# A hybrid decoder layer on eight cores: convolution gathered from a DRAM scratch, first weight slab requested first, norm two tiles ahead

## The chip, the cores and the metric

The kernel runs on all 8 cores of one Trainium2 chip. Each core has a matmul engine (TensorE, PE in the profile), VectorE (DVE), ScalarE (ACT), GpSimd (POOL) and SyncE (SP), and 16 DMA engines. There is no traffic between cores. The time is the device time of the slowest core, in microseconds. A comparison counts as faster or slower from 2% on.

## The reference

One layer of a decoder trunk, for 2 prompts of 8192 tokens and for 128 requests of 4 new tokens, D = 2048:

```python
n = _rmsnorm(hp, norm1_g[l])
q, k, v, u, g = _project(n, w_in[l], b_gate[l])        # u = ua * sigmoid(ub), gates = sigmoid
ya = _prompt_attention(q, k, v, sink[l])               # window 128, blocks of 128, sink column
ubuf = jnp.pad(u, ((0, 0), (CONV_W - 1, 0), (0, 0)))   # 31 taps, depthwise, 1024 channels
yc = _conv_tail(ubuf, conv_w[l], conv_b[l], cln_g[l], cln_b[l], w_conv_o[l])
hp = _finish(hp, ya, yc, g, w_attn_o[l], w_out[l], norm2_g[l], w_up[l], w_down[l])
...
def _finish(x, y_att, y_conv, gates, w_attn_o, w_out, norm2_g, w_up, w_down):
    ya = y_att @ w_attn_o
    mix = (gates[..., 0, :] * ya + gates[..., 1, :] * y_conv) @ w_out
    h = x + mix
    z = _rmsnorm(h, norm2_g) @ w_up
    return h + jnp.square(jax.nn.relu(z)) @ w_down
```

The sample requests go through the same steps, with cached keys, values and 30 cached convolution inputs each. The outputs are the final RMS norm of both, and the caches moved on by the new tokens.

## The kernel before

Each core computes 2048 prompt tokens and 64 sample tokens, channels on the partitions and tokens in the free dimension. It goes through them in three groups: 5, 6 and 5 blocks of 128 tokens; the first has a halo of 128 tokens more, the last the 64 sample tokens. A group passes through all layers before the next begins. The weights come anew for every group, in slabs of 2048 rows by 512 columns (2 MB in bf16, converted by the transfer), through three buffers `w0` to `w2`; `load_slab` requests the slab two ahead on GpSimd's queue when a stage begins. A slab serves 8 column tiles of 16 matmuls (`dense`), over two halves of the group's tokens (320, 384 and 352 columns in the three groups).

The stages of a group: `phase1` (RMS norm of the input, tile by tile, to `N`), `ua`, `kv`, `q`, `ub` (projections, of which `ua` and `ub` make the gated convolution input `u` in region `R2`), attention in units woven between these, then `conv_stage` woven between the first gate projections, `mix`, `out`, four pairs `up`/`dn` of the MLP, and `fin_stage`. All engines take their instructions in program order; `run(main, side, per)` sets that order by hand: after each step of the main stage it lets the side stage advance by `per` steps. Semaphore waits are derived from what each instruction reads and writes; `place` says which tiles of a region lie over which.

The convolution multiplies, per channel block of 128, a tile `X` with small weights `wd`: four groups of 32 channels, each with four shifted copies of `u` on the partitions, so that 8 matmuls cover 32 taps. `load_x` fills `X` by DMA from `u`, on SyncE's queue: 16 transfers per channel block, or 32 in the last group, where the sample tokens' `XS` comes too. `X` has four buffers, or two in the last group. `c`, the result, lies over `u` in region `R2`.

`phase1` of a later group runs beside the last down-projection, `dn_stage(G, 3)`, of the group before. Its step `front` squares an input tile (ScalarE), multiplies it by the norm's weights (GpSimd) and, in later groups, sums the squares over 16 blocks by halving (VectorE, into `ring`); its step `back` sums over partitions by a matmul with `onesD`, then takes root, reciprocal and product to `nT`. In the first group `back` sums by 16 matmuls of full width instead. The same down-projection also accumulates the squares of `h` for the final norm (`acc_stat`: ScalarE squares, GpSimd adds into `nS`).

The input copies that are outputs too (`ksn`, `vsn`, `csn`: caches shifted by four tokens) are requested in `consts`, on SyncE's queue, near the start.

## Time and profile before

| | us |
|---|---|
| median of 3 runs | 3978.87 |
| lowest, highest | 3974.25, 4410.77 |
| profiled execution, own time | 3986.84 |
| its span (slowest core, core 0) | 3985.4 |
| spans of the eight cores | 3947.3 to 3985.4 |
| TensorE busy | 3512.2 (88%) |
| VectorE, ScalarE, GpSimd busy | 1100.6, 879.9, 658.7 |
| matmuls in the chain that ended last | 72% |

The profile is of one execution, of the core that took longest. TensorE's busy time counts its matmuls at whatever clock was granted to it, so a busy stretch can still be slow. Every line of the program's work is recorded under one source line, L130, so groups are told apart by the names of their tiles: `MIX<-R` is the gather of `u` (in `R2`) into `X` (in `MIX`), `ps<-MIX,wd` are the convolution's matmuls, `ring` are the norm's sums.

### The profile page before, as it was taken

How to read it: one execution, taken by the hardware profiler on the slowest of the kernel's cores; microseconds unless marked ns; L12 is line 12 of the kernel's file. 1: busy time of each engine (PE TensorE's matmuls, PEld its weight loads, DVE VectorE, ACT ScalarE, POOL GpSimd, SP SyncE). 2: the span in 40 equal slices, each digit the busy share in tenths (PEclk: the TensorE clock that was granted, in tenths of full speed). 3: DMA queues.
4: the chain of work that ended last, by engine and by line, in shares of the span. 5: the costliest groups of instructions: out<-in, count | busy, mean ns of one | idle time of the engine just before them, and what ended most of it. 6: DMA issues, size and time to landing. Idle time of an engine off the chain costs nothing.

```text
span 3985.4 us, 62687 instructions; the slowest of 8 cores (3947.3 to 3985.4 us)
## 1 busy us (share of the span) xinstructions
PE 3512.2 (88%) x24352; PEld 2254.2 (57%) x24352; DVE 1100.6 (28%) x1936; ACT 879.9 (22%) x1955; POOL 658.7 (17%) x625
## 2 busy tenths in 40 slices
PE   3976999999988986999999999898535999999997
PEld 3644677677655543566666665464323666666664
DVE  2232222222245432312222222535203122222223
ACT  1243113100113343113210010314203113101103
POOL 3124012000023124003000001411112012000004
PEclk7998999999988998999999999788867999999998
DMA  8754689988876654569777677594423789888874
GB/s 157 115 99 85 97 149 141 124 115 125 120 137 140 105 92 79 76 97 165 103 104 98 99 106 118 97 171 69 90 69 51 106 145 130 108 110 117 106 110 97
DMA packets 389906, 440.98 MB, mean 111 GB/s; under 512 B 13584, under 2 KB 371600, under 8 KB 387216
## 3 DMA queue, kind: packets, MB, share of 16 engines
q0 software_dynamic: 347696, 355.68, 63.9%
q1 hardware_dynamic: 41920, 81.30, 7.2%
q8 instruction: 198, 3.24, 0.3%
q14 instruction: 92, 0.75, 0.1%
HBM read 752.81 MB, written 23.86 MB: 195 GB/s over the span
## 4 chain that ended last, share of the span: by engine, by line
PE 72%; SPq 6%; DVE 6%; ACT 5%; DMA 5%; issue 4%; POOL 0%; DVEq 0%; ACTq 0%; POOLq 0%
PE ps L130 72%; SPq L130 6%; DMA w<-w_up 3%; DVE R L130 2%; DVE MIX L130 2%; ACT TMP L130 2%; ACT P L130 1%; ACT R L130 1%; DVE TMP L130 1%; DMA MIX<-xf 1%; DMA wd<-wdx 1%; ACT MIX L130 1%; DMA w<-w_in 0%; DVE sm L130 0%; DVE GT L130 0%
## 5 line engine op out<-in xcount | busy, mean ns | idle before, releaser
L130 PE MATMUL ps<-N,w 128*128 128x384 bf16 (+3 forms) x11712 | 1809.3, 317 | 28.8 <-DMA w<-w_in 16.6
L130 PEld LDWEIGHTS ps<-N,w 128*128 128x128 bf16 x11712 | 1148.1, 99 | 681.3 <-issue 69.6
L130 PE MATMUL ps<-MIX,w 128*128 128x320 bf16 (+2 forms) x4608 | 688.8, 313 | 0.0
L130 PEld LDWEIGHTS ps<-MIX,w 128*128 128x128 bf16 x4608 | 450.9, 98 | 236.5
L130 PE MATMUL ps<-GT,w 128*128 128x320 bf16 (+2 forms) x3072 | 489.7, 325 | 0.0
L130 PEld LDWEIGHTS ps<-GT,w 128*128 128x128 bf16 x3072 | 311.3, 101 | 175.2 <-issue 10.0
L130 DVE SCALAR_TENSOR_TENSOR ring<-ps,TMP 128x320 f32<-128x320 f32 (+2 forms) x384 | 201.2, 525 | 703.9 <-PE ps L130 701.3
L130 DVE TENSOR_TENSOR R<-ps,R 128x320 f32<-128x320 f32 (+2 forms) x384 | 200.2, 524 | 636.5 <-PE ps L130 636.1
L130 PE MATMUL ps<-R,w 128*128 128x320 bf16 (+2 forms) x1536 | 261.3, 333 | 80.3 <-ACT GT L130 39.4
L130 PEld LDWEIGHTS ps<-R,w 128*128 128x128 bf16 x1536 | 155.8, 103 | 184.3 <-issue 101.4
L130 POOL TENSOR_TENSOR TMP<-TMP 128x320 f32<-128x320 f32 (+5 forms) x201 | 202.4, 1007 | 298.2 <-ACT TMP L130 295.6
L130 PE MATMUL ps<-MIX,wd 128*32 128x320 bf16 (+2 forms) x1792 | 87.3, 367 | 167.2 <-DMA MIX<-R 119.5
L130 ACT ACTIVATE TMP<-R 128x320 f32<-128x320 f32 (+5 forms) x264 | 136.1, 516 | 431.4 <-DVE R L130 422.0
L130 ACT ACTIVATE GT<-ring 128x320 bf16<-128x320 f32 (+2 forms) x192 | 95.3, 496 | 599.4 <-DVE ring L130 599.4
L130 ACT ACTIVATE MIX<-ring 128x320 bf16<-128x320 f32 (+2 forms) x192 | 94.9, 496 | 591.4 <-DVE ring L130 591.3
L130 DVE SCALAR_TENSOR_TENSOR GT<-GT,ps 128x320 f32<-128x320 f32 (+2 forms) x192 | 99.9, 520 | 402.7 <-PE ps L130 394.0
L130 ACT ACTIVATE GT<-ps,hbg 128x320 f32<-128x320 f32 (+2 forms) x192 | 106.1, 553 | 448.0 <-PE ps L130 448.0
L130 POOL DMA_DIRECT2D w<-w_dn x48 | 55.0, 1146 | 815.5 <-PE ps L130 815.5
L130 POOL DMA_DIRECT2D w<-w_up x48 | 55.3, 1152 | 703.1 <-PE ps L130 703.1
L130 PEld LDWEIGHTS ps<-MIX,wd 128*32 128x32 bf16 x1792 | 57.1, 119 | 197.9 <-issue 175.3
L130 ACT ACTIVATE P<-TMP,sm 128x129 bf16<-128x129 f32 (+1 forms) x264 | 107.9, 409 | 149.4 <-DVE sm L130 131.6
L130 POOL DMA_DIRECT2D w<-w_in x45 | 52.8, 1174 | 433.1 <-PE ps L130 396.2
(96 smaller groups left out, 1668.9 us busy)
## 6 DMA issues: line engine op xcount, KB each, us to landing
w<-w_up POOLq DMA_DIRECT2D x48, 2048.0 KB, 22.2
w<-w_dn POOLq DMA_DIRECT2D x48, 2048.0 KB, 17.0
w<-w_in POOLq DMA_DIRECT2D x45, 2048.0 KB, 16.8
w<-w_ac POOLq DMA_DIRECT2D x12, 2048.0 KB, 15.8
w<-w_out POOLq DMA_DIRECT2D x12, 2048.0 KB, 22.6
MIX<-xf SPq DMA_DIRECT2D x17, 1024.0 KB, 8.2
MIX<-R SPq DMA_DIRECT2D x256, 41.8 KB, 1.9
MIX<-R SPq DMA_DIRECT2D x128, 49.8 KB, 2.6
```

Source lines behind the costliest of these rows:

```text
L130: ins = getattr(engobj, fn[0])(*fn[1], **fn[2])
```

## The change

1. **Gather.** A stage `ub_stage` that has finished four channel blocks writes them to a DRAM scratch, `uscr` (`sscr` for the sample tokens). `load_x` reads from there, one transfer per shift for all four groups of channels: 4 per channel block, 8 in the last group. The first two `wd` are requested after the first `q` stage, and in the first two groups the loads of `X` are queued before attention's last units.
2. **Start.** The first weight slab is requested before the first tile is multiplied, the second after it; the constants and the cache copies come later.
3. **Norm.** `phase1` keeps three input buffers in all groups and a buffer for the squares of its own, in `AT`, a new tile that also holds attention's `P` and `PT`. `front` is two tiles ahead of `back`. In the first group every second tile is summed by halving.
4. **Cache copies** stand behind `up(1)` of groups 0 and 1.
5. **Final norm.** In groups 0 and 1 half of the additions of `acc_stat` move to VectorE, and the scale `gf` moves from ScalarE into VectorE's final multiplication. In the last group the last slab of the down-projection does all first halves before the second, and the first half's final norm starts under it. Outputs leave in stores of 2 or 4 channel blocks.

```diff
         def load_slab():
...
+        def prefetch(n):
+            while slab_at[1] < min(n, len(slabs)):
...
         def phase1(G):
-            place("MIX", [(f"x{i}", i * 8192, (i + 1) * 8192) for i in range(nx)] + ([] if first else [("xsq", 16384, 24576)]))
+            place("MIX", [(f"x{i}", i * 8192, (i + 1) * 8192) for i in range(3)])
+            place("AT", [("sq0", 0, 8192)])
...
-                if not first:
+                if not (first and i % 2 == 0):
                     for hw in (8, 4, 2, 1):
...
-            for i in range(min(nx, nt)):
+            for i in range(3):
                 load(i)
+            yield
             front(0)
+            yield
+            front(1)
             yield
             for i in range(nt):
                 back(i)
-                if i + nx < nt:
-                    load(i + nx)
+                if i + 3 < nt:
+                    load(i + 3)
                 yield
-                if i + 1 < nt:
-                    front(i + 1)
+                if i + 2 < nt:
+                    front(i + 2)
                     yield
...
         def ub_stage(G, hf):
+            hs = slice(hf * 4, hf * 4 + 4)
+            dmas("sp", [(uscr[G.g, hs, :, 0:G.UW].rearrange("k p c -> p k c"), G.uT[:, hs, :])],
+                 reads=[f"uT{c}" for c in range(hf * 4, hf * 4 + 4)], writes=[f"us{hf}"], sem=f"d_us{hf}")
...
             def load_x(ch):
                 i = ch % nb
                 pairs = []
-                for g in range(4):
-                    for tap in range(4):
-                        pairs.append((X[i][32 * tap:32 * tap + 32, g, :], G.uT[32 * g:32 * g + 32, ch, 1 + tap:1 + tap + L]))
...
+                for tap in range(4):
+                    src = uscr[G.g, ch].rearrange("(g c) w -> c g w", c=32)[:, :, 1 + tap:1 + tap + L]
+                    pairs.append((X[i][32 * tap:32 * tap + 32, :, :], src))
...
-        def acc_stat(G, src, rk, c, first):
+        def acc_stat(G, src, rk, c, first, dn=False):
+            eng = "dve" if dn and c else "pool"
...
+                    if G.last and fb == 3 and cb == 3 and c == 1:
+                        if mm_ == 1:
+                            fin_stat(G, 0)
+                        elif mm_ == 2:
+                            fin_rows(G, 0, 0, 4)
+                        elif mm_ == 3:
+                            fin_rows(G, 0, 4, 16)
...
-        for j in (1, 2):
-            slab_dep[j] = ["x0", "x1", "x2"]
+        slab_dep[1] = ["x0", "x1", "x2"]
         ph = phase1(Gs[0])
         next(ph)
+        prefetch(1)
+        next(ph)
+        prefetch(2)
+        drain(ph)
         consts()
-        drain(ph)
...
             dense_banks(4)
+            conv = conv_stage(G)
+            next(conv)
             att = att_stage(G)
...
+            if not G.SA:
+                next(conv)
             drain(att)
-            conv = conv_stage(G)
+            if G.SA:
+                next(conv)
...
+            if G.g == 0:
+                dmas("sp", [(ksn[:, :, :], ck[:, 4:128, :])], sem="d_o1")
+            if G.g == 1:
+                dmas("sp", [(vsn[:, :, :], cv[:, 4:128, :]), (csn[:, :, :], st[:, 4:30, :])], sem="d_o1")
```

GpSimd's order at the start, the piece of the difference (`w` are the weight slabs, `MIX<-MIX,vec` the multiplications of the six input tiles):

```order
-L130 TENSOR_TENSOR MIX<-MIX,vec 128x2048
+L130 DMA w<-w_in 128x16x512
+L130 TENSOR_TENSOR MIX<-MIX,vec 128x2048
+L130 DMA w<-w_in 128x16x512
+L130 TENSOR_TENSOR MIX<-MIX,vec 128x2048 x5
 L130 DMA msk<-masks 128x512
 L130 DMA smk<-smask 128x264
 L130 DMA idb<-ident 128x128
-L130 TENSOR_TENSOR MIX<-MIX,vec 128x2048 x5
-L130 DMA w<-w_in 128x16x512 x6
```

Two slabs move ahead of the multiplications, and the constants behind them.

SyncE's queue in the last group, from the attention's last transfers to the first channel block's gather, before:

```order
L130 DMA v_o<-GT 128x256
L130 DMA vs_o<-GT 64x256
L130 DMA MIX<-R 1x8x256 x8
L130 DMA u_o<-GT 128x768
L130 DMA MIX<-R 32x668
L130 DMA MIX<-R 32x512
```

and now:

```order
L130 DMA MIX<-R 1x8x256 x8
L130 DMA uscr<-R 128x4x672
L130 DMA sscr<-R 128x4x560
L130 DMA uscr<-R 128x4x672
L130 DMA sscr<-R 128x4x560
L130 DMA u_o<-GT 128x768
L130 DMA MIX<-uscr 32x4x668
L130 DMA MIX<-sscr 32x4x512
```

The pair `MIX<-R 32x668`, `32x512` stood there 128 times, the pair `MIX<-uscr`, `MIX<-sscr` stands 32 times, and the scratch writes stand ahead of the first.

VectorE's order in the norm stretch of the first group, one tile, before (`R<-ps,R` are the down-projection's additions, `MIX<-MIX` the halvings of the squares):

```order
L130 TENSOR_TENSOR MIX<-MIX 128x1024
L130 TENSOR_TENSOR MIX<-MIX 128x512
L130 TENSOR_TENSOR MIX<-MIX 128x256
L130 TENSOR_TENSOR ring<-MIX 128x128
L130 TENSOR_TENSOR R<-ps,R 128x320 x2
L130 RECIPROCAL ring<-ring 128x128
L130 TENSOR_TENSOR N<-MIX,ring 128x16x128
```

and now:

```order
L130 RECIPROCAL ring<-ring 128x128
L130 TENSOR_TENSOR N<-MIX,ring 128x16x128
L130 TENSOR_TENSOR R<-ps,R 128x320 x2
L130 TENSOR_TENSOR TMP<-TMP 128x320
L130 TENSOR_TENSOR AT<-AT 128x1024
L130 TENSOR_TENSOR AT<-AT 128x512
L130 TENSOR_TENSOR AT<-AT 128x256
L130 TENSOR_TENSOR ring<-AT 128x128
```

The halvings now belong to the tile two behind the one whose reciprocal stands ahead of them, and an addition of the statistics (`TMP<-TMP`) has joined every two additions of `h`.

## Rows read from the trace of the kernel before

**Rows 1.** Waits of TensorE, core 0: who was waited for; us in total, times, longest.

```profile
PE ps L130 <- DMA MIX<-R: 119.5, 11, 20.4
...
PE ps L130 <- DVE ring L130: 60.1, 12, 6.4
...
PE ps L130 <- DMA wd<-wdx: 24.3, 2, 12.2
```

**Rows 2.** Timeline, 0 to 100 us: start, us, engine, operation [idle before <-releaser].

```profile
2.92 0.88 SPq L130 DMA_DIRECT2D ksn<-ck  x1
...
11.05 1.91 ACT L130 ACTIVATE GT<-MIX 128x2048 f32<-128x2048 f32 x1
...
34.45 2.29 DVE L130 TENSOR_TENSOR N<-MIX,ring 128x2048 bf16<-128x2048 f32 x1
...
55.52 1.91 ACT L130 ACTIVATE GT<-MIX 128x2048 f32<-128x2048 f32 x1 [22.24 <-DMA MIX<-xf]
...
76.88 3.52 POOL L130 DMA_DIRECT2D w<-w_in  x3
...
93.98 6.20 PE L130 MATMUL ps<-N,w 128*128 128x336 bf16 x24 [16.59 <-DMA w<-w_in]
```

**Rows 3.** Timeline of the last group's gather, then that tile's requests and landings.

```profile
2832.19 169.21 SPq L130 DMA_DIRECT2D MIX<-R  x256
...
2855.70 4.89 PE L130 MATMUL ps<-MIX,wd 128*32 128x320 bf16 x96 [20.37 <-DMA MIX<-R]
...
2876.84 4.71 PE L130 MATMUL ps<-MIX,wd 128*32 128x320 bf16 x96 [13.67 <-DMA MIX<-R]
...
L130 SPq DMA_DIRECT2D MIX<-R x40: 507/591/1323, 2832.2 to 2859.4; - x40
...
DMA to landing us min/median/max: 1.8/5.4/6.2
```

**Rows 4.** Timeline of the first group's convolution.

```profile
291.52 4.46 PE L130 MATMUL ps<-MIX,wd 128*32 128x320 bf16 x64 [12.11 <-DMA wd<-wdx]
...
298.87 2.36 PE L130 MATMUL ps<-MIX,wd 128*32 128x320 bf16 x64
```

**Rows 5.** Timeline of the two norm stretches (1130 us, 2465 us), then 1181 us.

```profile
1171.50 10.36 PE L130 MATMUL ps<-GT,w 128*128 128x320 bf16 x64
...
1188.00 0.76 PE L130 MATMUL ps<-ring,onesD 128*128 128x128 f32 x2 [6.14 <-DVE ring L130]
...
2510.07 12.37 PE L130 MATMUL ps<-GT,w 128*128 128x384 bf16 x64
...
1181.69 5.77 DVE L130 TENSOR_TENSOR MIX<-MIX 128x1024 f32<-128x1024 f32 x3 [3.58 <-ACT MIX L130]
...
1181.73 4.65 POOL L130 TENSOR_TENSOR MIX<-MIX,vec 128x2048 f32<-128x2048 f32 x1 [1.53 <-ACT MIX L130]
```

**Rows 6.** Timeline of the end.

```profile
3929.72 25.97 PE L130 MATMUL ps<-GT,w 128*128 128x352 bf16 x173
...
3958.16 4.57 DVE L130 RECIPROCAL TMP<-TMP 128x352 f32<-128x352 f32 x2 [1.78 <-ACT TMP L130]
...
3962.64 16.16 DVE L130 TENSOR_TENSOR R<-R,TMP 128x352 f32<-128x352 f32 x22
```

**Rows 7.** Stretches: busy us by engine, clock, DMA share, GB/s; last row core 2.

```profile
550.00:700.00 150.00, 150.00 (x1103) 107.94 (x1101) 43.42 (x82) 44.67 (x95) 36.06 (x39) 1.00 0.97 152
...
1650.00:2450.00 800.00, 800.00 (x4921) 481.65 (x4920) 181.67 (x319) 123.96 (x233) 73.22 (x68) 1.00 0.75 110
...
2600.00:2650.00 50.00, 50.00 (x287) 31.46 (x286) 22.85 (x40) 11.01 (x24) 6.97 (x7) 0.81 0.88 191
...
2600.00:2650.00 50.00, 50.00 (x352) 34.57 (x351) 25.25 (x46) 11.27 (x25) 8.85 (x9) 1.00 0.92 194
```

**Rows 8.** Requests: KB each, median us to landing.

```profile
ksn<-ck SPq DMA_DIRECT2D x1, 1984.0 KB, 25.4
```

**Rows 9.** The page, costliest groups: count | busy us, mean ns | idle before.

```profile
L130 DVE TENSOR_TENSOR R<-ps,R 128x320 f32<-128x320 f32 (+2 forms) x384 | 200.2, 524 | 636.5 <-PE ps L130 636.1
```

More of the change, by code:

```diff
@@ L231, in build @@
         tf = TMP[:, :]
+        Pb = [AT[:, i * 520:(i + 1) * 520].rearrange("p (g c) -> p g c", g=4) for i in range(4)]
+        PT = [AT[:, 2080 + i * 1024:2080 + (i + 1) * 1024] for i in range(2)]
+        atf = AT[:, :].bitcast(F32)
         seq = {}
@@ L252, in load_slab @@
             slab_at[0] += 1
-            while slab_at[1] < min(i + 3, len(slabs)):
+            prefetch(i + 3)
+            return i % 3
+        def prefetch(n):
+            while slab_at[1] < min(n, len(slabs)):
                 j = slab_at[1]
@@ L395, in back @@
                 b = bank("d")
-                if first:
+                if first and i % 2 == 0:
                     for kc in range(16):
-                        do("pe", "matmul", ["ones", "xsq"], [f"ps{b}"], inc=(kc == 15), out=ps[b][:, 0:w], lhsT=onesD[:, :],
-                           rhs=sqf[:, kc * w:(kc + 1) * w], start=(kc == 0), stop=(kc == 15))
+                        do("pe", "matmul", ["ones", f"sq{i % ns}"], [f"ps{b}"], inc=(kc == 15), out=ps[b][:, 0:w], lhsT=onesD[:, :],
+                           rhs=sqs[i % ns][:, kc * w:(kc + 1) * w], start=(kc == 0), stop=(kc == 15))
                 else:
@@ L531, in conv_stage, with load_wd @@
         def conv_stage(G):
+            def load_wd(ch):
+                dmas("pool", [(wd[ch % 2][:, :, :], wdx[ch])], writes=[f"wd{ch % 2}"], sem=f"d_wd{ch % 2}")
+            load_wd(0)
+            load_wd(1)
+            yield
             L = G.TP + 28
@@ L540, in conv_stage, with load_x @@
                 XS.append(mxb[:, o + 4 * L:o + 4 * L + 2048].rearrange("p (g r b) -> p g r b", g=4, b=16) if G.SA else None)
+            def load_x(ch):
+                i = ch % nb
+                W = 800
+                pairs = []
+                for tap in range(4):
+                    src = uscr[G.g, ch].rearrange("(g c) w -> c g w", c=32)[:, :, 1 + tap:1 + tap + L]
+                    pairs.append((X[i][32 * tap:32 * tap + 32, :, :], src))
+                    if G.SA:
+                        src = sscr[ch].rearrange("(g c) w -> c g w", c=32)[:, :, 16 * tap:16 * tap + 512]
+                        pairs.append((XS[i][32 * tap:32 * tap + 32, :, :, :].rearrange("p g r b -> p g (r b)"), src))
+                dmas("sp", pairs, reads=[f"us{ch // 4}"] + ([f"ss{ch // 4}"] if G.SA else []), writes=[f"X{i}"], sem=f"d_X{i}")
+            for ch in range(nb):
+                load_x(ch)
+            xl = nb
+            yield
             place("TMP", [("S1", 0, 3072), ("S2", 3072, 6144), ("cq0", 6144, 7680), ("cq1", 7680, 9216)])
@@ L635, in att_stage @@
         def att_stage(G):
+            place("AT", [(f"P{i}_{g}", i * 1040, (i + 1) * 1040) for i in range(4) for g in range(4)]
+                  + [(f"PT{i}", 4160 + i * 2048, 4160 + (i + 1) * 2048) for i in range(2)])
             place("TMP", [(f"sp{i}", i * 2064, (i + 1) * 2064) for i in range(2)])
@@ new lines, in dn_stage, with store_y, fin_rows @@
+                    yield
+        def store_y(G, m, k, c0, n):
+            dmas("sp", [(yT[m:m + k, :, G.off + c0:G.off + c0 + n].rearrange("k p c -> p k c"), G.h[:, m:m + k, c0:c0 + n])],
+                 reads=[f"h{j}_{c}" for j in range(m, m + k) for c in range(2) if c * G.NM // 2 < c0 + n and c0 <= c * G.NM // 2],
+                 sem=f"d_y{nxt('y', 8)}")
+        def fin_rows(G, c, m0, m1):
+            _, R = stat_views(G)
+            c0, n = G.ch[c]
+            for m in range(m0, m1):
+                hv = G.h[:, m, c0:c0 + n]
+                do("dve", "tensor_tensor", [f"h{m}_{c}", f"nR{c}"], [f"h{m}_{c}"], out=hv, in0=hv, in1=R[:, c0:c0 + n], op=ALU.mult)
+                if m % 4 == 3 and (m < 12 or c == 0):
+                    store_y(G, m - 3, 4, c0, n)
+                elif m > 11 and m % 2 == 1 and c == 1:
+                    store_y(G, m - 1, 2, c0, n)
@@ L968, in fin_stage @@
                     hv = G.h[:, m, c0:c0 + n]
-                    do("pool" if G.last and m % 3 == 2 else "dve", "tensor_tensor", [f"h{m}_{c}", f"nR{c}"], [f"h{m}_{c}"], out=hv,
-                       in0=hv, in1=R[:, c0:c0 + n], op=ALU.mult)
-                dmas("sp", [(yT[m, :, G.off:G.off + G.NM], G.h[:, m, :])], reads=[f"h{m}_0", f"h{m}_1"], sem=f"d_y{m % 8}")
+                    do("dve", "scalar_tensor_tensor", [f"h{m}_{c}", f"nR{c}", "vec"], [f"h{m}_{c}"], out=hv, in0=hv,
+                       scalar=vec[:, V_GF + m:V_GF + m + 1], in1=R[:, c0:c0 + n], op0=ALU.mult, op1=ALU.mult)
+                if m % 2 == 1:
+                    store_y(G, m - 1, 2, 0, G.NM)
                 yield
```

73 lines of the change are left out of this document (29 added, 44 removed).

## The prediction

> **What bounds the kernel now.** The page says that TensorE is busy for 3512 us of 3985 and that 72% of the chain that ended last is its matmuls, so I looked for the 470 us in which it is not, and for the stretches in which it runs slow. I read the list of what TensorE waited for first [rows 1]: on the gathered convolution input 119.5 us, on VectorE's `ring` sums of the next group's norm 60.1 us, on the convolution weights `wd` 24.3 us. Then the windows by 50 us showed where. Four places stand out. The first dense matmul starts at 93.98 us [rows 2]. The last group's convolution waits once per channel [rows 3]. The two stretches in which a group's last down-projection runs beside the next group's norm wait once per 128-token tile [rows 5]. And the end has 30 us with no dense matmul [rows 6]. Between these TensorE never stops: 800 us on end at a granted clock of 1.00, the upper level, 2.4 GHz [rows 7]. The change touches all four places and leaves the dense work between them alone.
>
> **The change, part by part.** The profiled execution took 3986.84 us: a span of 3985.4 and 1.4 around it. That is 8 us above the median of the three runs, 3978.87; I make the sum against 3986.84 and take off 4 at the end, as half of that difference.
>
> *Start.* Now ScalarE squares tile 0 at 11.05, and three tiles are done at 34.45 + 2.29 = 36.7, so 8.6 us a tile. The next three inputs were requested behind the three cache copies, and ScalarE waits 22.24 us for them, until 55.52. The first weight slab is requested by GpSimd only at 76.88, behind all six tile multiplications, and TensorE waits 16.59 us for it [rows 2]. After: no copies ahead, slab 0 requested first, slab 1 behind one tile. Both waits go. What is late next is the tile chain itself: from 11 us, six tiles at 8.6 give 63; the change puts two tiles in flight and takes the 16 passes of TensorE away from every second tile, and then VectorE and GpSimd, some 6 to 7 us a tile by the same steps, give 48. I take 52, nearer the lower since every step except TensorE's is overlapped with another tile: 42 us gained, 31 to 46 by the two ends. The slab now travels beside the first inputs; if it delayed them by half of the 16.59 that it takes alone, the gain would be 8 less.
>
> *Gather, last group.* `load_x` issues 32 requests per channel. 256 of them occupy SyncE's queue for 169.21 us, 0.66 each, 21.1 us a channel [rows 3], against about 7 us of TensorE work a channel. Seven waits of TensorE add to 20.37 + 6 x 13.9 = 103.8, and another of 18.9 stands behind ScalarE's copy into `c`, whose space the gather still reads: 122.7 us. After each wait the matmuls start at half speed: 64 of them take 4.46 against 2.36 without a wait [rows 4]; eight times about 1.5 is 12. The change issues 8 requests per channel, each four times as large. The trace has no request of that shape. The nearest rows are the 32-partition ones at 0.59 median and one contiguous 2 MB copy at 0.88 [rows 2, 3]: 4.7 to 7 us a channel; if the price went by rows moved it would be 4 x 0.59, or 19 us, the same as now. I take 0.6, since the 2 MB copy shows that bytes do not set it. Landing takes 5.4 more. With two buffers a channel comes every (4.7 + 5.4 + 4)/2 = 7.1 us, against 6.4 for convolution and gate matmuls, so 5 us in all remain, plus a first wait of about 9 (scratch write, issue, landing, since only one gate group is left as cover) and 6 of slow clock. Gain 135 - 20 = 115; 20 if the price goes by rows, 125 at best.
>
> *Gather, first two groups.* Here waits are 119.5 - 103.8 = 15.7 for the input, 24.3 for `wd` [rows 1], which was requested behind a weight slab and is now requested a stage earlier, some 3 behind ScalarE, and about 13 of slow clock: 56. But all inputs now leave SyncE behind the second scratch write, which waits for the last gated channel; before, the first four channels were gathered while the projection ran. So a wait of 7 to 9 us appears in each group where `wd` was waited for, with 2 to 4 behind it and some slow clock: 27 together. Gain 29, between 10 and 40.
>
> *Scratch traffic.* Six writes of 0.7 to 0.8 MB and two of 0.6 are new, and nothing waits for them except those first loads; costed there. The Trainium skill speaks against this part: DMA: Bandwidth & Descriptors, section Why small descriptors are slow (HBM only), says that small descriptors lose rate when DRAM is one side and not from SBUF to SBUF, and this gather becomes DRAM to SBUF with 1336-byte rows. No row here shows such a read; what hangs on it is the 5.4 us of landing alone, and if that doubled, a channel would come every 9.8 us and the last group's gain would be 96 instead of 115.
>
> *Norm beside the down-projection.* Now one tile costs 10.36 of 64 matmuls, 6.14 of waiting and 0.56: 17.06 us, of which about 9.3 is needed at full clock [rows 5]. Six tiles lose about 44. With 384 columns a batch takes 12.37 where 10.6 would do, and the waits are 5 to 4: about 37. After, VectorE's sums stand two steps ahead of the matmul that reads them, so TensorE does not wait for a tile but for VectorE's total load. Per tile: 5.77 for the halvings, which run as long as GpSimd's 4.65 multiplication beside them lasts, 2.29 for the normalised tile, four additions of 0.52 and two of the statistics that move over from GpSimd [rows 2, 5, 9], and an estimated 2.5 for the small steps and for waiting on ScalarE's squares: 13.7 us, against 9.3 and 10.9 of TensorE. Six tiles fall behind by 26 and 17 us; eight PSUM banks let TensorE run about 14 ahead. That leaves 12 and 3. Gain 32 + 34 = 66. Bounds: 30, if half of each wait survives, and 78.
>
> *End.* The last dense matmul ends at 3929.72 + 25.97 = 3955.7, and then come two reciprocals (4.57), 22 multiplications on VectorE in 16.16 [rows 6] and the last store, to 3985.4: 29.7 us. After, columns are finished in two halves. The first half's statistics come under the last matmuls; 12 of its 16 multiplications, one reciprocal and the second half's 16 stand behind: 12 x 0.52 + 2.3 + 16 x 0.52 + 4 for the last store = 21. Gain 9, between 3 (at 0.73 a multiplication, as in the row) and 11.
>
> *Cache copies, at their new place.* SyncE has nothing to wait for once the last residual is requested, so the first copy leaves near 610 us, under the output projection, whatever its line in the program. There the DMA engines are busy 0.97 of the time [rows 7], and the copy takes 25.4 us to land [rows 8]. Weight slabs have about 15 us in hand. I take a loss of 5 us, bounds 0 and 20. Two copies in the second group meet a share near 0.8 with slack: nothing, up to 10.
>
> *At nothing:* the final scale by `gf` that leaves ScalarE and enters VectorE's multiplication (same instruction count on VectorE, next to dense matmuls), stores of two channels blocks at once, `P` and `PT` in one tile `AT`.
>
> Sum: 42 + 115 + 29 + 66 + 9 - 5 = 256. 3986.8 - 256 = 3730.8; less 4, 3727.
>
> **The rivals.** *Requests are priced by rows.* Then the last group keeps its period near 19 us and the first two become bound by SyncE too. For it: a 32-partition request of 1.3 KB rows already costs as much as one of 8 KB rows on 128 partitions, so something else than bytes is counted. Against it: that same comparison holds for rows. Time: gather gains 20 + 0, so 3850. *The load moves to VectorE and the DMA engines.* The norm stretches gain only 30, the first copy costs 20, the start 31: 3727 + 36 + 15 + 11, so about 3790. *The saving is larger:* norm 78, gather 165, start 46, end 11, copies 0: 3727 - 44 = 3683. *The clock falls as the cores get denser.* On core 0 it was 0.81, between the two levels, from 2600 to 2650 us, with TensorE busy throughout and 287 matmuls done where core 2 at 1.00 did 352 [rows 7]: 1.23 times the time. It decides from the length: it outweighs the 256 gained once it holds over 1110 us of what is now full speed. If it held over 1600 us, 3727 + 368 = 4095, slower than before. Against it: the 800 us at 1.00 [rows 7] are dense already and run at the upper level, on the other seven cores as on this one. The Trainium skill (TensorE: Matmul & The Clock Gate, Part 1) states just this as the rule, 13/16 of the clock once three cores of a die run dense matmuls; this trace disagrees over most of its length, so the rule carries no more than this small chance.
>
> **How the numbers follow.** The sum as it stands, within 3685 to 3775: 0.66. The larger load on VectorE and DMA, 3775 to 3800: 0.12. The larger saving, under 3685: 0.09. Price by rows, 3800 to 3870: 0.08. Clock, slower than 3979: 0.03; unforeseen, near no change: 0.02. The range 3680 to 3800 holds the first two and a little of the third, 8 in 10. A measurement of this kernel can tell 2%, 80 us, from no change: faster than 3899 has 0.95, within 0.02, slower 0.03.
>
> **What would show it.** In the changed profile: the first `N,w` matmul near 52 us; 64 requests for the last group's `X`, 0.6 us each, and its eight convolution batches 7 us apart; the norm stretches with waits of 0 to 2 us per tile and VectorE busy over 0.8; 21 us from the last dense matmul to the end; a wait for `w_up` or `w_out` after 610 us of no more than 5. The prediction is wrong if a request of four rows per partition takes over 1 us, if the `X` loads land over 10 us after their issue, or if the granted clock of the dense stretches leaves 1.00.

## The result, and the profile after

The changed kernel takes **0.971 of the time before (95% interval 0.966 to 0.976)**: 3851 and 3865 us against 3968 to 3979. I had said 3727, range 3680 to 3800. The sign is right, the gain about half of what I worked out: in the profiled executions 3986.84 became 3851.42, 135.4 us in place of 256. (Comparisons leave out executions in which the cores of one half of the chip, or of both, ran at a lower clock; for e4, e5 and e10 too few were left, and times stand without an interval.)

First the list of what TensorE (PE) of core 0 waited for, in the changed kernel:

```profile
engine line waited for: us in total, times, longest us
PE ps L130 <- DVE ring L130: 85.8, 13, 35.0
...
PE ps L130 <- DMA MIX<-sscr: 37.3, 6, 26.9
PE ps L130 <- DMA w<-w_up: 35.0, 5, 19.3
PE ps L130 <- DMA MIX<-uscr: 32.3, 3, 16.4
...
PE ps L130 <- DMA w<-w_out: 7.4, 1, 7.4
PE ps L130 <- DMA wd<-wdx: 6.0, 4, 2.9
```

Against [rows 1], the gathered input fell from 119.5 us to 69.6 (two names now, `uscr` and `sscr`) and `wd` from 24.3 to 6.0; `ring` rose from 60.1 to 85.8, but 44.7 of that are two waits at the start, shown next; beside the down-projections it fell to 39.8. The waits for the slabs of `w_up` and `w_out`, 10.3 before, are now 42.4.

*The start.* TensorE's and then GpSimd's timeline, to be laid beside [rows 2] (start, length, instruction, and in brackets the idle time before it with what ended it):

```profile
59.05 0.77 PE L130 MATMUL ps<-ring,onesD 128*128 128x128 f32 x2 [35.03 <-DVE ring L130]
60.29 5.69 PE L130 MATMUL ps<-AT,onesD 128*128 128x128 f32 x32 [0.47 <-ACT AT L130]
75.66 0.77 PE L130 MATMUL ps<-ring,onesD 128*128 128x128 f32 x2 [9.68 <-DVE ring L130]
76.22 4.69 PE L130 MATMUL ps<-N,w 128*128 128x336 bf16 x16
```

```profile
18.02 1.20 POOL L130 DMA_DIRECT2D w<-w_in  x1 [2.47 <-DMA MIX<-xf]
43.32 7.17 POOL L130 TENSOR_TENSOR MIX<-MIX,vec 128x2048 f32<-128x2048 f32 x2 [24.10 <-DMA w<-w_in]
```

The first dense matmul is at 76.22, not 52. GpSimd waits 24.10 us for a *weight slab* before it may multiply an input tile. `slab_dep[1]` names `x0`, `x1`, `x2` as read by the slab's transfer, to hold it back; the multiplication writes `x1`, so the program makes it wait for that reader. SyncE waited for the same slab: the load of the fourth input tile, into the space of `x0`, left at 43.29.

*The last group's convolution*, against [rows 3], on TensorE, and in the line of windows below it the 25 us in which TensorE did nothing (the last three numbers are TensorE's granted clock, the DMA engines' share and GB/s):

```profile
2792.41 2.56 PE L130 MATMUL ps<-N,w 128*128 128x352 bf16 x16
2821.86 4.43 PE L130 MATMUL ps<-MIX,wd 128*32 128x320 bf16 x96 [26.89 <-DMA MIX<-sscr]
...
2828.71 2.61 PE L130 MATMUL ps<-MIX,wd 128*32 128x320 bf16 x96
...
2837.41 4.89 PE L130 MATMUL ps<-MIX,wd 128*32 128x320 bf16 x96 [3.59 <-DMA MIX<-sscr]
...
2845.74 2.61 PE L130 MATMUL ps<-MIX,wd 128*32 128x320 bf16 x96 [0.75 <-ACT GT L130]
```

```profile
2795.00:2820.00 25.00, 0.00 (x0) 0.00 (x0) 0.00 (x0) 0.56 (x1) 0.00 (x0) 0.57 1.06 202
```

The price of a request held: 0.43 us once the engines had room. The first wait didn't: 26.89 us where I had 9. Scratch writes, a slab of `w_ac`, an output store and the first loads share the engines in that gap, which run at a share of 1.06. SyncE's queue shows it as requests that take up to 3.4 us:

```profile
2793.30 0.36 SPq L130 DMA_DIRECT2D uscr<-R  x1
2793.75 0.47 SPq L130 DMA_DIRECT2D sscr<-R  x1
...
2810.96 3.38 SPq L130 DMA_DIRECT2D MIX<-sscr  x1
...
2827.72 0.43 SPq L130 DMA_DIRECT2D MIX<-sscr  x1
```

*A norm tile* on VectorE beside the down-projection, against [rows 5]:

```profile
1198.50 0.94 DVE L130 RECIPROCAL ring<-ring 128x128 f32<-128x128 f32 x1
1199.54 2.29 DVE L130 TENSOR_TENSOR N<-MIX,ring 128x2048 bf16<-128x2048 f32 x1
1201.75 0.88 DVE L130 TENSOR_TENSOR R<-ps,R 128x320 f32<-128x320 f32 x2
1203.37 0.96 DVE L130 TENSOR_TENSOR TMP<-TMP 128x320 f32<-128x320 f32 x1 [0.74 <-ACT TMP L130]
1205.17 5.77 DVE L130 TENSOR_TENSOR AT<-AT 128x1024 f32<-128x1024 f32 x3 [0.84 <-ACT AT L130]
1211.04 0.29 DVE L130 TENSOR_TENSOR ring<-AT 128x128 f32<-128x128 f32 x1
1211.25 0.88 DVE L130 TENSOR_TENSOR R<-ps,R 128x320 f32<-128x320 f32 x2
1212.87 0.95 DVE L130 TENSOR_TENSOR TMP<-TMP 128x320 f32<-128x320 f32 x1 [0.74 <-ACT TMP L130]
1213.74 0.94 DVE L130 RECIPROCAL ring<-ring 128x128 f32<-128x128 f32 x1
```

From reciprocal to reciprocal 15.24 us, where I had 13.7 and TensorE needs 9.3. VectorE is busy for 13.0 of them and waits for ScalarE for 2.3.

*The weights*: the first up-projection batch of the second group, and the output projection ahead of it as a window (clock, DMA share and GB/s last):

```profile
1887.59 4.11 PE L130 MATMUL ps<-N,w 128*128 128x384 bf16 x16 [19.31 <-DMA w<-w_up]
```

```profile
1785.00:1868.00 83.00, 83.00 (x513) 49.91 (x511) 18.40 (x33) 31.85 (x62) 32.63 (x33) 1.00 1.00 181
```

A share of 1.00 while TensorE runs at full pace: the stretch looks covered, and the bill comes one stage later. The share alone doesn't tell of it, though: in the kernel before, the first group's output projection (574 to 644 us) ran at 1.03, and the first batch behind it waited for nothing.

**Where the 135 us are**, from the starts of the same batches in both timelines (core 0, after minus before): at the first gate batch 258.04 - 274.89 = -16.9; behind the first convolution 397.93 - 418.23 = -20.3; at the last down-projection of the first group -1.4; at the second group's gates -17.2; behind its convolution 1597.71 - 1622.14 = -24.4; at its third down-projection 2389.42 - 2393.03 = -3.6; at the third group's gates 2792.41 - 2830.38 = -38.0; behind its convolution 2961.15 - 3088.21 = -127.1; at its last down-projection -130.0; at the end -135.6. Twice some 20 us that were gained are gone again behind the output projection. From the end of the convolution to the last down-projection the second group took 854.1 us on every core before and 867 to 875 after; the first took 715 to 737 before and 729 to 741 after, which is 19 us more on core 0 and nothing on core 4.

### The profile page after: what moved, and what is told of

It reads as the page before. It is cut to its first block, busy times and chain, and to the rows that moved or that the text cites. A ratio compares the mean times of both kernels' runs of the same rounds, so it can differ in the third digit from the quotient of the medians.

```text
span 3849.8 us, 61954 instructions; the slowest of 8 cores (3825.3 to 3849.8 us)
## 1 busy us (share of the span) xinstructions
PE 3462.5 (90%) x24262; PEld 2226.1 (58%) x24262; DVE 1150.0 (30%) x1988; ACT 841.0 (22%) x1891; POOL 618.9 (16%) x585
## 4 chain that ended last, share of the span: by engine, by line
PE 75%; DMA 8%; DVE 6%; ACT 5%; issue 4%; SPq 1%; another core or an unknown queue 0%; POOL 0%; DVEq 0%; ACTq 0%; POOLq 0%
PE ps L130 75%; DMA w<-w_up 4%; ACT AT L130 2%; DVE R L130 2%; DVE AT L130 2%; ACT TMP L130 2%; DVE TMP L130 1%; DMA MIX<-sscr 1%; ACT R L130 1%; DMA MIX<-uscr 1%; SPq L130 1%; DMA wd<-wdx 1%; DMA w<-w_in 1%; DVE GT L130 1%; DMA MIX<-xf 1%
## 5 line engine op out<-in xcount | busy, mean ns | idle before, releaser
L130 PE MATMUL ps<-GT,w 128*128 128x320 bf16 (+2 forms) x3072 | 473.8, 318 | 0.0
L130 PEld LDWEIGHTS ps<-R,w 128*128 128x128 bf16 x1536 | 154.1, 102 | 167.7 <-issue 85.8
L130 POOL TENSOR_TENSOR TMP<-TMP 128x352 f32<-128x352 f32 (+5 forms) x171 | 175.1, 1024 | 319.7 <-ACT TMP L130 318.4
L130 PE MATMUL ps<-MIX,wd 128*32 128x320 bf16 (+2 forms) x1792 | 72.1, 322 | 76.4 <-DMA MIX<-sscr 37.3
L130 ACT ACTIVATE AT<-TMP,sm 128x129 bf16<-128x129 f32 (+1 forms) x264 | 107.9, 409 | 149.5 <-DVE sm L130 131.7
L130 DVE TENSOR_TENSOR TMP<-TMP 128x320 f32<-128x320 f32 (+2 forms) x36 | 35.4, 983 | 274.3 <-ACT TMP L130 273.2
## 6 DMA issues: line engine op xcount, KB each, us to landing
MIX<-uscr SPq DMA_DIRECT2D x32, 199.0 KB, 13.5
```

Of the source, the lines that this page charges most:

```text
L130: ins = getattr(engobj, fn[0])(*fn[1], **fn[2])
```

## The experiments

All start from the changed kernel unless said otherwise.

**The false reader.** Label e1_reader.

```
-dmas("pool", ..., reads=slab_dep.pop(j, []), writes=[f"w{j % 3}"], ...)
+dmas("pool", ..., after=slab_dep.pop(j, []), writes=[f"w{j % 3}"], ...)   # waits as before, isn't entered as a reader
```

> The changed kernel with one edit: the second weight slab still waits for the three input tiles, but is no longer entered as a reader of them, so that GpSimd's multiplication of tile 1 doesn't wait for the slab (24.10 us in the changed kernel). Theory (this wait is why the start gained 17 and not 42): the first dense matmul comes at 48 to 55 us instead of 76, and the whole is 20 to 28 us shorter, near 3827. Rival (the start is bound by what the DMA engines bring: inputs and slabs share them, so the wait only moves to the input tiles or to the slab): first dense matmul at 65 to 75 us, and 0 to 10 us shorter.

0.971 (0.966 to 0.976), as without the edit. The 24.10 us wait is gone, and the first dense matmul comes at 69.92, 6.3 earlier only. ScalarE's timeline tells why:

```profile
28.40 0.28 ACT L130 ACTIVATE ring<-ps 128x128 f32<-128x128 f32 x1 [8.38 <-PE ps L130]
40.36 1.91 ACT L130 ACTIVATE GT<-MIX 128x2048 f32<-128x2048 f32 x1 [11.68 <-DMA MIX<-xf]
```

The fourth input tile was waiting underneath: with three buffers its load leaves only when the first tile is normalised (30.74), and lands at 40. That tile had become late itself: VectorE's halvings for the second tile, 2.55 us in the changed kernel, took 10.69 beside GpSimd's multiplications, which now came at once, and the first tile's product stands behind them. My theory was half right; of the rival the numbers fit (first dense matmul at 65 to 75 us, 0 to 10 us shorter), but its cause, what the DMA engines bring, is only a part. The 6 us aren't seen at the end, where they would be within the interval: the waits for `w_out` and `w_up` in the first group were 17 to 34 us over the cores, against 12 to 24.

**The cache copies.** e2_copies.

```
 load_x(xl)
 xl += 1
+if xl == 8:
+    dmas("sp", [[ksn copy], [vsn copy], [csn copy]][G.g], sem="d_o1")
```

> The changed kernel with the cache copies at another place: one in each group, issued behind the last load of the convolution's input, where few weight slabs are wanted. Theory (the copies take the DMA engines from the weight slabs under the output projection and the up-projection): TensorE's waits for w_up and w_out fall from 42.4 us to under 8, and the whole is 30 to 38 us shorter, near 3817. Rival (the slabs are late there since the denser kernel asks for more per us, and the copies only stand beside it): the waits stay above 25 us, and the whole changes by less than 12 us. A third possibility: the copies now delay slabs of the gates behind the convolution, with a new wait for w_in or w_ac of 5 to 15 us there.

0.967 (0.962 to 0.972). In the second group the theory holds on all eight cores: 8 to 19 us of waits for `w_up` and `w_out` become 0. The third possibility, a new wait for `w_in` or `w_ac`, appears on no core. In the first group the theory holds for some cores only. Core 0 and core 3, first group, waits of TensorE from 560 to 1180 us:

```profile
PE ps L130 <- DMA w<-w_up: 2.4, 1, 2.4
```

```profile
PE ps L130 <- DMA w<-w_up: 29.4, 9, 9.4
```

What core 0 gains doesn't show in the kernel's time, which is that of the slowest core; 0.967 and the changed kernel's 0.971 can't be told apart. The waits go by neighbours: 2 and 6 us on cores 0 and 1, 27 and 29 on 2 and 3, 12 and 14, 37 and 34 on 6 and 7. The spans, of the first four cores:

```profile
core 0: 3818.8 us, clock 0.954
core 1: 3808.9 us, clock 0.955
core 2: 3860.8 us, clock 0.951
core 3: 3868.0 us, clock 0.950
```

In other executions of this kernel another pair is the late one. The waits don't explain all of the spread: core 7 waited 34 us and took 3845, core 4 waited 12 and took 3849. Nor is the new place free: in the mean over the cores the first convolution, from the gates to its end, took 9 us more than in the changed kernel, the second 7.

**The order on SyncE's queue.** e3_xfirst.

```
-(write of the second half of uscr/sscr, store of u_o)   in ub_stage(G, 1)
 next(conv)                                              # loads of the first channels, now ahead of ub_stage's write
+G.write()                                               # that write and store, behind them
```

> The changed kernel with the order on SyncE's queue turned round: the loads of the first four (last group: two) channels come ahead of the write of the second half of the scratch, which they don't need. Theory (the first wait of each convolution is the queue: the loads stand behind writes that wait for the last gated channel, and behind their bytes): first waits of 14.4 and 16.4 us in the first two groups fall to 0 to 3, that of 26.9 us in the last group to about 12, since its buffers come free only when attention ends; together 40 us shorter, near 3811. Rival (the DMA engines are full there anyway, with the weight slab that was asked for just before, and the later channels pay what the first ones gain): waits for the loads of the later channels grow by as much as the first ones shrink, and the whole is 0 to 12 us shorter.

0.967 (0.964 to 0.971), again not to be told from the changed kernel. The first waits of all three convolutions went to 0, and most of it was taken back: on core 0 the three convolutions wait 57 us for input and `wd`, where the changed kernel's wait 76. In the first group the wait is

```profile
258.75 2.36 PE L130 MATMUL ps<-MIX,wd 128*32 128x320 bf16 x64
...
284.26 4.18 PE L130 MATMUL ps<-MIX,wd 128*32 128x320 bf16 x64 [16.31 <-DMA wd<-wdx]
```

for `wd` (13.8 in the second group), and in the last for the third channel's input (20.59 us). In the last group the DMA engines ran at a share of 1.07 to 1.09 from 2806 to 2830 us, and the requests behind the write took up to 5.05 us each: there the rival describes it. For `wd` a second account stands untested, the order on GpSimd's queue. The `wd` in question was requested at 261.70, 5 us behind a slab of `w_ac` (256.74) on that queue; the slab landed at 282.7 and `wd` 1.3 us after it. In the changed kernel a `wd` requested at 279.86, when the slab before it was nearly in, landed at 288.8, again 1.9 us after the slab. What the convolution keeps of the gain is lost behind it: the stretch from there to the last down-projection takes 746 to 760 us in the first group against 729 to 741 in the changed kernel.

**VectorE beside GpSimd.** e4_gamma.

```
-do("pool", "tensor_tensor", ..., out=x, in0=x, in1=gamma broadcast, op=mult)
+for kc in range(16): do("act", "activation", ..., out=x[:, kc, :], in_=x[:, kc, :], func=Copy, scale=gamma[kc])   # groups 2 and 3
```

> The changed kernel with the multiplication by the norm's weights in the last two groups' norm moved from GpSimd (one instruction of 4.65 us a tile) to ScalarE (16 a tile). Theory (VectorE sets the pace of a tile, 15.2 us, and its halvings are long because GpSimd works beside them): the four halvings of a tile fall from 6.06 us together to 2.5 to 4, a tile takes 11.5 to 13 us, and each of the two stretches is 12 to 20 us shorter: near 3820. Rival (the halvings take their time by themselves, or what paces a tile is the chain between the engines): halvings as before, a tile at 15 us or more, since ScalarE has some 4 to 6 us more a tile, and the whole between 5 us shorter and 15 longer.

3881 and 3894 us, no gain (the kernel before took 3979 to 4000 beside it). Yet the halvings shrank as the theory said (first group's stretch):

```profile
1191.11 2.55 DVE L130 TENSOR_TENSOR AT<-AT 128x1024 f32<-128x1024 f32 x3 [0.84 <-ACT AT L130]
1193.77 0.29 DVE L130 TENSOR_TENSOR ring<-AT 128x128 f32<-128x128 f32 x1
1193.98 0.88 DVE L130 TENSOR_TENSOR R<-ps,R 128x320 f32<-128x320 f32 x2
1199.73 0.95 DVE L130 TENSOR_TENSOR TMP<-TMP 128x320 f32<-128x320 f32 x1 [4.87 <-ACT TMP L130]
```

5.77 became 2.55, and VectorE then stood 4.87 us behind ScalarE's 16 new instructions (7.80), for a statistic that the norm doesn't need. A tile took 16.2 us, and the whole came out as the rival had it (what paces a tile is the chain between the engines). That the two engines take turns can be read from the changed kernel too: GpSimd's multiplication takes 3.60 us where VectorE is idle (11.95 us) and 4.65 beside the halvings, and at 1205 us the halving of 1024 columns took 1.23 us, the one of 512 columns 3.91 and the one of 256 columns 0.43, so one of them waits and not all run slower. The Trainium skill (SBUF — State Buffer, Terms, "shared port pair") says that VectorE and GpSimd lock one pair of ports against each other for a whole instruction. By that rule one halving waits out the multiplication, and these rows agree.

**The statistics back on GpSimd.** e5_stat: `acc_stat(G, hv, ..., m == 0)` without the last argument.

> The changed kernel with the additions of the final statistics given back to GpSimd (as in the kernel before), the norm still two tiles ahead. With the multiplication on ScalarE the halvings fell from 5.77 to 2.55 us and a tile still took 16.2 us, since VectorE stood 4.87 us per tile behind ScalarE's squares. Theory (VectorE takes its instructions in order, and the two additions per tile that wait for ScalarE's squares, 0.74 us each and 0.95 long, hold up the halvings behind them; without them a tile costs 5.77 + 0.29 + 0.94 + 2.29 + 4 x 0.52 = 11.4 us): a tile at 11.5 to 13.5 us instead of 15.2, TensorE's waits for the sums from 20 and 15 us in the two stretches to under 8 each, and the whole 15 to 25 us shorter. Rival (the additions on GpSimd work beside VectorE's halvings and lengthen them as the multiplication does, and GpSimd becomes late itself): a tile at 14 us or more, and the whole 0 to 8 us shorter.

3867 and 3881 us, beside 4011 to 4012 for the kernel before. A tile: 14.65 us; the two stretches are 101 to 103 and 105 to 107 us long, 2 us shorter each. VectorE's waits on the statistics went and 2.58 us for ScalarE's square of the tile itself appeared. The tile fits the rival (14 us or more) but not for its reason, since the halvings kept their 5.77: the chain between the engines has several links of nearly the same length.

**Half the weights' bytes.** e7_half and e8_beforehalf, one edit in each kernel:

```
-dmas("pool", [(wsl[j % 3][:, :, :], slabs[j])], ...)
+h = 8 if j % 55 >= 19 and j > 2 else 16      # w_out, w_up, w_dn
+dmas("pool", [(wsl[j % 3][:, 0:h, :], slabs[j][:, 0:h, :])], ...)
```

> The changed kernel with the slabs of w_out, w_up and w_dn moved by half: only the first 8 of 16 blocks of rows are loaded, the other half of the buffer keeps older weights, so the output is not the reference's. TensorE's work is the same. Theory (in the output and up-projections the slabs come at what the DMA engines can move, so that whatever is gained ahead of that stretch is partly spent there): all of TensorE's waits for w_out and w_up go (27 to 42 us on the cores of the changed kernel), and the whole is 30 to 42 us shorter. Rival (these waits come from the order of the requests, each behind the multiplications that free its buffer, not from bytes): the waits stay above 15 us and the whole changes by under 10 us.

> The kernel before, with the same slabs moved by half (output not the reference's). It says what the change is worth once weights are no bound. Theory (the change gained more than the whole shows, and paid part of it in waits for weights, of which the kernel before had 5 to 18 us): this kernel is only 5 to 18 us shorter than the kernel before, so that the change is worth 155 to 175 us between the two halved kernels instead of 115 to 135. Rival (both kernels are held by the weights alike): both shorten by the same, and the change is worth 115 to 135 us here too.

0.949 (0.947 to 0.951) and 0.989 (0.986 to 0.992): 3807 to 3809 and 3968 to 3969 us. No core waits for `w_out` or `w_up` in either, so the rival of e7 (waits above 15 us) falls. The change is worth 3968 - 3808 = 160 us between the halved kernels, as the theory of e8 said (155 to 175), and not 115 to 135. Each step by itself was larger than expected, however. The halved kernel before is 43 us under the 4011 to 4012 that the kernel before took beside it, where 5 to 18 were expected; e7_half is some 70 us under the changed kernel's 3874 to 3882 on the same chip, though not beside it, where 30 to 42 were. The stretches show where it lies. From the end of the convolution to the last down-projection every core of both halved kernels takes 713.9 us in the first group and 854.1 in the second. The changed kernel takes 729 to 741 and 867 to 875 in its first profile, 725 to 765 and 865 to 875 in r1_after. On core 0 of the first profile that is 26 and 21 us lost to weights, where the waits were 20 and 19: the matmuls behind a wait start at a lower clock (16 of them took 4.4 us instead of 2.3). The cores of e7_half lie within 14 us of each other (3792 to 3806 in the profiled execution) where those of e2_copies spread over 59 and those of the changed kernel over 24.

**The residual input.** e11_nores: `load_res(m + 8)` left out.

> The changed kernel without the loads of the residual input for the upper 8 of 16 blocks of channels (each group reads 8 blocks and uses them twice, so the output is not the reference's): 2.6, 3.1 and 2.9 MB less during the output projections. Theory (the output projection asks more of the DMA engines than they can move: four weight slabs at about 16 us of all engines each, 5 MB of residual input and a 2 MB cache copy within 70 to 83 us, and the waits for w_out and w_up behind it pay that off): those waits fall by 10 to 20 us in each of the first two groups, and the whole is 20 to 35 us shorter than the changed kernel beside it. Rival (only the weights' own rate or the cache copies count, the residual loads are small beside them): waits within 5 us of those of the changed kernel, the whole within 8 us.

0.963 (0.959 to 0.967), 3850 and 3853 us, beside 0.970 (0.967 to 0.973), 3874 to 3882 us, for the changed kernel on the same chip (r1_after):

> The changed kernel itself, unchanged, so that the three kernels beside it have it on the same chip. Every theory expects its ratio to the kernel before again, 0.965 to 0.976, with TensorE's waits for w_out and w_up in the first group at 10 to 40 us on every core.

Some 26 us shorter, inside the expected 20 to 35. Waits for weights over the cores: second group 0 to 12 (changed kernel 8 to 16), first group 12 to 29 (9 to 40). In the mean over the cores they fell by 6 us in each group, short of the expected 10 to 20, and the two stretches behind the convolutions became 4 and 9 us shorter, which is half of the 26. So the output projection's own traffic counts: copies, residual input and slabs together.

**Another norm.** e10_norm: statistics on GpSimd, the multiplication on ScalarE in two bursts of 8, ScalarE's square a step early.

```
 back(i); load(i + 3)
+front(i + 2)      # Square, first 8 multiplications
 yield
+halve(i + 2)      # last 8 multiplications, then the halvings
 yield
```

> The changed kernel with another order in the norm of the second and third group: statistics on GpSimd, the multiplication by the norm's weights on ScalarE in two bursts of 8, and ScalarE's square of a tile one step ahead of the halvings that read it. With the statistics alone on GpSimd a tile still took 14.65 us: 5.77 for the halvings beside GpSimd's multiplication, and 2.58 in which VectorE waited for ScalarE's square. Theory (VectorE's chain paces a tile; both of these go): VectorE needs 2.55 + 0.29 + 0.94 + 2.29 + 1.76 and a wait of 0.9 = 8.7 us, ScalarE 7.8 + 1.9 + 1.9 = 11.6, so a tile takes 11 to 12 us, TensorE's waits for the sums in the two stretches together fall from 35 us to under 15, and the whole is 20 to 30 us shorter than the changed kernel beside it. Rival (what is gained in the first stretch is taken back by the engines' other waits, or ScalarE's bursts hold up the square roots as they did with 16 in a row): a tile at 14 us or more, within 8 us of the changed kernel.

3838 us (one execution) against 3874 to 3882: 36 us or more, above the expected 20 to 30. On VectorE of core 0 two tiles take 1209.65 - 1184.24 = 25.4, so 12.7 us each, where 11 to 12 was expected; TensorE's waits for the sums in both stretches are 12 us together (40 in the changed kernel). The stretches themselves tell more than one execution's time: on cores 0 to 3 they are 85 to 88 and 89 to 92 us long, against 104 to 105 and 107 to 108 in r1_after, 35 us together.

**All that helped.** First e9_best (reader, order, copies, statistics), then e12_all (the same with e10_norm's norm).

> The changed kernel with four edits at once: no false reader at the start, the loads of the first channels ahead of the second scratch write, the cache copies behind the convolution's last load, the statistics back on GpSimd. By the single runs each gives its own place less: the start 7 us, the first waits of the convolution 15 a group but paid back by waits for wd and slabs, the copies 19 us in the second group on all eight cores and an uneven amount in the first. Theory (what is gained ahead of the first group's output projection is taken back there, later gains stay): 3800 to 3830 in place of 3851, the slowest core being one that waits for w_up in the first group by 20 us or more. Rival (the gains add up): 25 + 40 + 34 + 20, so 3740 or less.

> The changed kernel with all edits that gained at their own place: no false reader, first channels' loads ahead of the second scratch write, cache copies behind the convolution's last load, and the norm of e10_norm. The first three with the statistics on GpSimd gave 0.9527 of the kernel before on another chip. Theory (edits behind the first group's output projection add up, since nothing there is bound by weights): 15 to 25 us shorter than that, a ratio of 0.946 to 0.950. Rival (the first group's wait for weights takes the first stretch's gain only in part, and the second stretch alone counts): 0.950 to 0.954.

e9_best: 0.953 (0.950 to 0.956), 3815 to 3829 us, as its theory said, and the slowest core is one that waits 26 us for `w_up` in the first group. e12_all: **0.951 (0.948 to 0.953)**, 3797 to 3804 us, which is faster than the kernel before and 77 us, 2.0%, under the changed kernel on the same chip, at the edge of what counts as faster. It can't be told from e9_best, and its theory (0.946 to 0.950) and rival (0.950 to 0.954) are both left standing. The gains don't add up. In e12_all core 0 begins its first convolution at 251 us, 24 earlier than the changed kernel; behind it the lead is 6 (392.08 against 397.93). It is 18 at the first down-projection (772.17 against 790.20), where the waits for weights have been shorter so far, and gone at the last (1140.69 against 1137.93). The windows of that stretch, and the waits for `wd` (250 to 400 us) and for `w_up` (400 to 920 us):

```profile
250.00:400.00 150.00, 97.34 (x956) 61.28 (x955) 36.84 (x63) 45.53 (x82) 42.61 (x40) 0.80 0.56 95
400.00:550.00 150.00, 150.00 (x1106) 108.06 (x1105) 35.25 (x72) 23.73 (x45) 9.87 (x9) 1.00 0.92 125
550.00:920.00 370.00, 351.57 (x2533) 250.16 (x2532) 81.81 (x160) 75.18 (x161) 47.77 (x50) 0.97 0.93 127
```

```profile
PE ps L130 <- DMA wd<-wdx: 20.5, 2, 16.7
```

```profile
PE ps L130 <- DMA w<-w_up: 18.4, 5, 7.7
```

Another 7.25 us follow at 1017. What stays is gained behind that stretch: the two norm stretches are 86 to 89 and 87 to 90 us long on all eight cores, as in e10_norm.

## Why the prediction was wrong, by its own steps

The sign was right, and so were the places where time was gained; the sum was 120 us too large. Two steps failed in their mechanism. The copies under the output projection were priced at 5 us, and the stretches behind it lost 40. The start was said to be held by the tile chain alone; a wait that the change itself brought held it, and beneath that the buffer of the fourth input, 25 us together. In the norm and the gather the mechanism was right and the sizes were not (29 and 44 us too much). Term by term:

- **Start, 42; measured 17.** The step that failed is "Both waits go. What is late next is the tile chain itself". A new wait of 24.10 us came with `slab_dep[1]`, which stood in the diff: I read it as "behind one tile" and didn't ask who writes what the slab's request is said to read. e1_reader shows a second one beneath it, the fourth input, whose load needs the first tile's buffer and so waits for VectorE.
- **Gather, last group, 115; measured 89** (-38.0 to -127.1). On the eight cores 86 to 92. Price per request (0.43 against my 0.6) and period (7.6 us a channel against 7.1) were as predicted, so the rival "priced by rows" is out. Mis-sized is "a first wait of about 9": 26.9, while the DMA engines ran at 1.06; the later waits added 10 where I had 5. Landing was 7.2 us at the median in this group instead of 5.4, so it did not double; the measured 89 lies below the 96 of a doubled landing because of the first wait. In the first two groups it was 12.0 and 13.5, over the 10 us that I had named as a sign of being wrong. The Trainium skill (DMA: Bandwidth & Descriptors, Why small descriptors are slow (HBM only)) says that transfers from SBUF to SBUF don't pay for small descriptors as those with DRAM on one side do; the late landings here came with full engines, in e3_xfirst too, and no run separates row length from load.
- **Gather, first two groups, 29; measured 3.4 + 7.2 = 11.** "7 to 9 us" at the first channel was 14.4 and 16.4, with the engines at a share near 1 there too (0.93 to 1.12 from 260 to 280 us).
- **Norm, 66; measured 37**: 119.5 to 104.6 in the first stretch, 129.9 to 107.4 in the second. VectorE does pace a tile, and 13.7 was 15.2: the two additions of statistics took 0.95 us each, not 0.52, and the small steps with the waits 3.5 us, not 2.5. At 15.2 six tiles fall 35 us behind in the first stretch, not 26; TensorE waited 24.7 of them, so the allowance of 14 us for the PSUM banks was about 11. e4, e5 and e10 show why a count of busy time falls short: VectorE takes its work in order and stands behind ScalarE, so what is taken from one link is partly paid at the next. And some 6 of the second stretch's 22.5 us aren't the norm's: cores 0 and 1 of the kernel before took 129.9 us there at a granted clock of 0.78 (2500 to 2600 us), cores 2 to 7 took 122.6 to 124.1 at 0.86 to 0.90.
- **End, 9; measured 5.6.** 23.5 us from the last dense matmul where I had 21. TensorE's last wait, 4.90 for GpSimd's last statistic, is not the reason: VectorE was busy until 3834.9 with the 12 multiplications anyway. Missing from my sum are 2.6 us until those began (VectorE still had four multiplications and an addition ahead of them), and the last store took 5.5, not 4; the 16 multiplications took 7.1 instead of 8.3.
- **Copies, -5; measured -19.0 and -20.8**, the term most wrong. "Weight slabs have about 15 us in hand" stood on no row, and took a 2 MB copy by itself. In the second group taking the copies away removes the waits on every core (e2_copies), and less residual input shortens them (e11_nores); in the first the output projection and what follows wait for weights with the copies or without (e2), unless the slabs are halved (e7), which gives core 0 back 26 us there and 21 in the second. The rival that named this load put 20 us on the first copy and nothing on the second.
- **Not in the sum:** 2.9 us fewer waits for `w_up` in the last group, and 12.9 between the norm and the gates (0.9 in the second group, 12.0 in the third), the latter from the clock: core 0 was at 0.81 from 2600 to 2700 us before (573 matmuls) and at 0.97 in the like stretch after (658 from 2580 to 2680). Only cores 0 and 1 had it: they took 224 us from the norm to the third group's gates, the other six 211 to 215, and all eight 212 in the changed kernel. With the 6 us above, some 18 of core 0's 135 are thus a slow stretch of the one execution profiled before and not the change's doing.

16.9 + 89.1 + 10.7 + 37.4 + 5.6 - 39.8 + 2.9 + 12.9 = 135.7. Left open: why one pair of cores waits 30 us and another 3 in the same execution; whether row length or load sets the landing of the gather's loads; and whether `wd` in e3_xfirst waits for full engines or for its place on GpSimd's queue.

## What to carry over

Put a ledger of DMA time beside the one of the engine that bounds the kernel. Here the output projection kept the DMA engines full (1.00 to 1.06) while TensorE ran on, and 19 to 21 us of what had been gained ahead of it were spent on waits for weights a stage later, once two megabytes or so of copies had been put there. Look for that cost on all cores: another one may be the slowest. When a dependency is used to delay something, ask who writes the thing it claims to read; here two engines stood behind it. And for an engine that takes its instructions in order, add up the waits of the whole chain for one tile, not its busy time.

## What the runs showed of the hardware

- Waits for weights come in pairs of neighbouring cores: 2/6, 27/29, 12/14 and 37/34 us on cores 0/1, 2/3, 4/5 and 6/7 in the first group of e2_copies, 26/23, 11/13, 12/9 and 28/24 in that of e12_all; with half the bytes no core waits. The Trainium skill (HBM Reference, Specifications (TRN2)) says that two cores share one domain of DRAM; the pairs agree with it, but no run here had one of a pair idle.
- A request on SyncE's queue took 0.43 us when the DMA engines had room (a share of 0.5 to 0.9) and up to 5.05 at a share of 1.07: the queue's time was then a symptom of load.
- VectorE's three large halvings of a tile: 5.77 us beside a GpSimd instruction of 4.65, 10.69 beside two at the start of e1_reader, 2.55 without. Of the 5.77 it was one halving, 3.91 us long, that stood.
- The granted clock of TensorE was 1.00 for 800 us on end on all eight cores at once, with no pause in the matmuls (second group: 854.1 us on each core); 0.81 was seen on cores 0 and 1 for 100 us in the same execution.
